# Eight norms of a four-layer fp32 kernel: token half 1 goes to TensorE unscaled, against a diagonal matrix

## The reference

```python
def rms_norm(x, g):
    xf = x.astype(jnp.float32)
    y = xf * lax.rsqrt(jnp.mean(xf * xf, axis=-1, keepdims=True) + RMS_EPS)
    return (y * g.astype(jnp.float32)).astype(x.dtype)
...
h = rms_norm(x, norm_g[l, 0])
...
x = x + rms_norm(h, norm_g[l, 1])
h = conv_ffn(rms_norm(x, norm_g[l, 2]), w_up[l], conv_w[l], conv_b[l], w_down[l])
x = x + rms_norm(h, norm_g[l, 3])
```

## Time and profile before

| | |
|---|---|
| median of 3 runs | 1632.51 us (1631.99 to 1634.74) |
| the profiled execution | 1632.15 us, of which the span of the trace is 1630.4 us |
| TensorE busy | 1531.6 us, 94% of the span |
| VectorE busy | 961.3 us, 59% |
| ScalarE busy | 784.4 us, 48% |
| mean granted TensorE clock | 0.945 of full speed |

### The profile page before, as it was taken

One profiled execution on the slowest core, in us unless ns is written; L12 is line 12 of the kernel. 1 busy time (PEld: TensorE's weight loads), 2 busy tenths in 40 slices (PEclk: granted clock), 3 DMA queues, 4 the chain that ended last, 5 costly groups with the idle time before them and its releaser, 6 DMA issues.

```text
span 1630.4 us, 24600 instructions
## 1 busy us (share of the span) xinstructions
PE 1531.6 (94%) x9621; PEld 1369.2 (84%) x9621; DVE 961.3 (59%) x1438; ACT 784.4 (48%) x1250; POOL 58.2 (4%) x78
## 2 busy tenths in 40 slices
PE   5897999998799998998999989999999999899998
PEld 5865988985699997888999979879999687789997
DVE  6547342235666768556676756575555575655555
ACT  5424321331555557546555656454445455454443
POOL 5002000000000000000000000001000100000000
PEclk9887897996899998999999999999999999999999
DMA  9320000004365553416556545445555445045550
GB/s 290 107 68 0 1 1 1 1 1 143 123 193 193 179 190 129 156 45 215 187 179 201 181 153 183 155 157 181 184 188 195 156 157 179 18 158 188 180 193 39
DMA packets 135063, 222.07 MB, mean 136 GB/s; under 512 B 6137, under 2 KB 105697, under 8 KB 134720
## 3 DMA queue, kind: packets, MB, share of 16 engines
q1 hardware_dynamic: 132688, 214.19, 39.7%
q0 software_dynamic: 2144, 6.61, 1.3%
q10 hardware_dynamic: 144, 0.06, 0.0%
HBM read 219.77 MB, written 1.05 MB: 135 GB/s over the span
## 4 chain that ended last, share of the span: by engine, by line
PE 86%; DVE 8%; ACT 4%; issue 1%; DMA 0%; SPq 0%; DVEq 0%; ACTq 0%
PE ps L446 84%; DVE ulo L432 1%; DVE scratch L1772 1%; PE ps L743 1%; ACT uhi L424 1%; DVE x_sb L1746 1%; DMA raw<-in_w_rkv 0%; DVE scratch L2020 0%; DVE scratch L1852 0%; PE ps L1062 0%; DVE xs L1722 0%; DVE xn_lo L1734 0%; ACT scratch L1290 0%; DVE x_sb L1752 0%; ACT scratch L1388 0%
## 5 line engine op out<-in xcount | busy, mean ns | idle before, releaser
L432 DVE TENSOR_TENSOR ulo<-raw,uhi 128x1024 fp32r<-128x1024 f32 x400 | 492.7, 1235 | 394.6 <-ACT uhi L424 394.3
L424 ACT ACTIVATE uhi<-raw 128x1024 fp32r<-128x1024 f32 x400 | 422.7, 1058 | 449.3 <-PE ps L446 446.3
L446 PE MATMUL ps<-xn_hi,uhi 128*128 128x256 f32 x1472 | 420.6, 286 | 10.7 <-DVE xn_lo L1786 7.7
L446 PE MATMUL ps<-xn_hi,ulo 128*128 128x256 f32 x1472 | 419.3, 285 | 0.0
L446 PE MATMUL ps<-xn_lo,uhi 128*128 128x256 f32 x1472 | 419.2, 285 | 0.0
L446 PEld LDWEIGHTS ps<-xn_hi,uhi 128*128 128x128 f32 x1472 | 285.3, 194 | 14.4 <-issue 9.9
L446 PEld LDWEIGHTS ps<-xn_lo,uhi 128*128 128x128 f32 x1472 | 285.3, 194 | 1.7
L446 PEld LDWEIGHTS ps<-xn_hi,ulo 128*128 128x128 f32 x1472 | 284.8, 193 | 0.0
L446 PE MATMUL ps<-scratch 128*128 128x128 f32 (+6 forms) x1248 | 208.9, 326 | 14.5 <-DVE scratch L2033 9.0
L446 PE MATMUL ps<-uhi,xm_hi 128*128 128x512 f32 x512 | 201.5, 394 | 1.8 <-DVE xm_lo L1968 1.1
L446 PEld LDWEIGHTS ps<-scratch 128*128 128x128 f32 (+3 forms) x1248 | 174.0, 209 | 34.6 <-DVE scratch L2033 10.4
(11 more groups left out here) (271 smaller groups left out, 1420.5 us busy)
## 6 DMA issues: line engine op xcount, KB each, us to landing
raw<-in_mlp_w SPq DMA_DIRECT2D x64, 1024.0 KB, 5.3
raw<-in_w_up SPq DMA_DIRECT2D x44, 1024.0 KB, 5.1
raw<-in_w_down SPq DMA_DIRECT2D x22, 1024.0 KB, 4.8
raw<-in_gmlp_w_in SPq DMA_DIRECT2D x16, 1024.0 KB, 5.2
raw<-in_fox_w_in SPq DMA_DIRECT2D x16, 1024.0 KB, 5.0
raw<-in_w_rkv SPq DMA_DIRECT2D x12, 1024.0 KB, 10.5
raw<-in_gmlp_w_out SPq DMA_DIRECT2D x8, 1024.0 KB, 4.9
raw<-in_w_o_rwkv SPq DMA_DIRECT2D x4, 1024.0 KB, 5.9
```

What stands on the lines that cost most here:

```text
L424: nc.scalar.activation(ring_unit(uhi, m, n), raw_unit(n, j), ACT.Copy).then_inc(hi_done, 1)
L432: nc.vector.tensor_tensor(ring_unit(ulo, m, n), raw_unit(n, j), ring_unit(uhi, m, n).bitcast(F32), ALU.subtract).then_inc(lo_done, 1)
L446: return nc.tensor.matmul(o, l, r, start=start, stop=stop, skip_group_check=True)
```

## The change

For token half 1, DVE no longer writes the scaled half into `xs`. It writes a new 128x128 fp32 tile `diag`, the identity with each row multiplied by that token's reciprocal root. PE then computes for each piece the product of `x_sb` (as the stationary operand, by which it comes out transposed) with `diag`, so that transposing and scaling are one product in fp32. Half 0 stays as it is, a scaling and eight transpositions. `xs_done` counts two events for each norm instead of three.

```diff
+        diag = sb("diag", [P, P])
...
             def norm(n, e):
                 for tok in range(NT):
-                    pe.wait_ge(xs_done, 3 * n + tok + 1)
+                    pe.wait_ge(xs_done, 2 * n + tok + 1)
                     for b in range(4):
-                        if tok == 1 and b == 2:
-                            pe.wait_ge(xs_done, 3 * n + 3)
                         for f in range(2):
                             c = (2 * b + f) * P
-                            last = nc.tensor.transpose(bank(b, P, T * f + P * tok), xs[:, tok, c:c + P], ident[:, :])
+                            o = bank(b, P, T * f + P * tok)
+                            if tok == 0:
+                                nc.tensor.transpose(o, xs[:, 0, c:c + P], ident[:, :])
+                            else:
+                                last = mm(o, x_sb[:, 1, c:c + P], diag[:, :], True, True)
                         if tok == 1:
                             last.then_inc(tr_done, 1)
...
                     step(nc.vector.reciprocal(stat[:, 4 + tok:5 + tok], stat[:, 2 + tok:3 + tok]))
-                    for c in ((slice(0, D),), (slice(0, D // 2), slice(D // 2, D)))[tok]:
-                        TS(xs[:, tok, c], x_sb[:, tok, c], stat[:, 4 + tok:5 + tok], None, ALU.mult).then_inc(xs_done, 1)
+                    if tok == 0:
+                        TS(xs[:, 0, :], x_sb[:, 0, :], stat[:, 4:5], None, ALU.mult).then_inc(xs_done, 1)
+                    else:
+                        TS(diag[:, :], ident[:, :], stat[:, 5:6], None, ALU.mult).then_inc(xs_done, 1)
```

## The result

The changed kernel takes 1640.08 us (median of 6 runs, 1637.65 to 1642.73) against 1631.89 us for the kernel before (6 runs beside it): the ratio is 1.0049, with a 95% interval of 1.0036 to 1.0062, or about 8 us slower. I had forecast 1634.9 us, with a range up to 1638.0. The direction was right. The size, +8.2 us against my +2.4, was more than three times mine.

A forecast was written before the change was run, and what follows sets the result against it. TensorE, busy 1531.6 of 1630.4 us, was taken to bound the kernel. Later first products at the norms, +3.8 us, less 1.4 for a sooner clock made +2.4: 1634.9 us, range 1631.5 to 1638.0.

The forecast's parts named there:

- A product of fp32 leaves two records and costs two transpositions: Half-1 pieces on TensorE: each product takes 0.428 us at low clock or 0.23 at full, against 0.217 and 0.117.
- VectorE's saving is covered: Half-1 scaling: VectorE is 0.63 us ahead, hidden by TensorE's transpositions, and can show only at norms 6 and 7.
- Norm 0 costs nothing: Norm 0: ScalarE's copies of transposed x cover the extra products; 0, up to +0.2 us.
- The sum of +3.8 us over norms 1 to 5 and 7: Later first products: +0.85, +0.84, +0.68, +0.42 and +0.65 us at norms 1 to 5, +0.35 at norm 7.
- The clock gives some back: After norm 2: no idle hole before the products, so full clock returns one 3.4 us stretch sooner; -1.4 us.
- Norm 6, full clock. 0: Norm 6: TensorE's stream ends before the old start of products; 0, between -0.15 and +0.1 us.
- the first (the clock gives nothing back, +3.8 to +5.5): Clock gives nothing back, each norm costs what is listed or a little more; 1636.3 to 1638 us, chance 0.30.
- the second rival: All norms: nothing is hidden, every product's extra counts; +10.3 us, 1642.8 us, chance 0.04 (over +5.5).
- a sign of being wrong: Whole kernel: low-clock time, 5.5% x 2 x 1630, changing by more than one or two stretches would refute the forecast.
- slower by over 0.2%: Whole kernel: a time above 1635.8 us, given chance 0.32.
- The third rival: Five low norms: clock returns a stretch sooner, as products or an unbroken stream count more; -4.7 us, 1627.8, chance 0.06.

The follow-up runs named there:

- transpose_unscaled: The changed kernel with half 1 turned by transpose operations instead of products, its scaling left out; 1630.72 us, ratio 0.9994 to the kernel before.
- diag_0: The kernel before with the change at norm 0 alone; 1632.17 us, ratio 0.9997.
- transpose_twice: The kernel before with each half-1 piece transposed twice in a row; 1635.21 us, ratio 1.0020.
- product_ident: The kernel before with half 1, still scaled by VectorE, turned by fp32 products with the identity at all norms; 1637.72 us, ratio 1.0039.
- diag_6_7: The kernel before with the change at norms 6 and 7 alone; 1632.94 us, ratio 1.0007.
- diag_6: The kernel before with the change at norm 6 alone; 1632.17 us, ratio 1.0007.
- the filled kernels: Kernel before and changed kernel, each with spare identity products ahead of norms 1 to 7; 1625.56 and 1626.78 us (before, two sets), 1626.66 us (changed).
- diag_1_3: The kernel before with the change at norms 1 to 3 alone; 1633.99 us, ratio 1.0010.
- diag_4_7: The kernel before with the change at norms 4 to 7 alone; 1636.29 us, ratio 1.0025.
- the filled changed kernel: The changed kernel with spare identity products into an unread bank ahead of norms 1 to 7; 1626.66 us, ratio 0.9981 to the kernel before.

## Why the prediction was wrong

- **A product of fp32 leaves two records and costs two transpositions: right.** 128 records, 0.209 us each at the low clock.
- **VectorE's saving is covered: right at norms 1 to 5.** `transpose_unscaled` keeps that saving whole, and its stretches 1 to 5 are those of the kernel before to 0.04 us. At norm 6 its first product starts 0.24 us sooner, within the 0.2 to 0.3 that I had for half 1.
- **Norm 0 costs nothing: right** (`diag_0`, ratio 0.9997).
- **The sum of +3.8 us over norms 1 to 5 and 7: right as a sum, and there by luck.** The mean lengths of the stretches over the 11 profiles without fill, with the change or one transposition per piece (so without `transpose_twice` and `product_ident`), with the change at that norm less without it, are +0.71, +0.68, +0.86, +1.04, +0.05 and +0.40: +3.7. Norm 4 cost 0.6 more than its 0.42, because the clock stayed low there for 6.8 us instead of 3.4 in the changed kernel, and norm 5 cost 0.6 less than its 0.65, because there it wasn't low at all. In `product_ident`, where the clock was low at norm 5 too, stretch 5 took 186.7 us, about 1 us more than in the kernel before.
- **"The clock gives some back", -1.4 us: this step failed.** What I foresaw happened in the profile: after norm 2 the clock is back at 648.3 us, 3.6 us sooner after the start of the stretch, and stretch 2 is 0.7 us shorter than before. But norms 4 and 6 each have 3.4 us more at the low clock and norm 5 has 3.4 less, so that with norm 2 the time at the low clock around the norms is 34 us before and after: what one norm gets back another loses. And I had taken one profile of the kernel before for the rule. Among the six profiles without the change at norm 2, stretch 2 took 104.2 to 107.0 us: the kernel gets its clock back early in half of them by itself. One such, `diag_6_7`:

```profile
638.93:743.18 104.25, 91.79 (x584) 81.62 (x584) 65.98 (x160) 61.02 (x152) 0.00 (x0) 0.96 0.30 102
```

  With the change it took 106.3 us in all five. Against the mean of the others, 105.6, the change costs +0.7 at norm 2 instead of giving 0.6.
- **"Norm 6, full clock. 0": this step failed too.** At the full clock it is nothing on the spot: the first product starts 0.04 us later in `diag_6` and in the filled kernels. But the changed kernel met norm 6 at the low clock in all three of its profiles, and the first product came 1.0 to 1.1 us later. The whole stretch, the last attention layer with it, is +2.5 us in the mean of the profiles (standard error 1.1), and `diag_6` alone measured +1.3 (0.7). I had put no term at all for the clock of a layer behind a norm.
- 3.7 + 2.5 + 0.2 (up to norm 1) = 6.4 us by profiles, against 7.2 in the mean of the runs. Taking back the -1.4 and adding norm 6 accounts for most of the miss; the terms after norm 6 and up to norm 1 are known to 1 us at best. Of the rivals, the first (the clock gives nothing back, +3.8 to +5.5) had the mechanism at the norms; its bound of 5.5 was too low, since none of my cases let the clock of a later layer fall. By its number the result lies where I had put the second rival (over +5.5, chance 0.04), but that one's mechanism is not what happened: it wanted 1.7 us at each low norm, and the stretches show at most 1.0.
- I had named as a sign of being wrong that the time at the low clock changes by more than one or two stretches of 3.4 us. It came: 181.7 us in the profile of the kernel before, 202.9 in the first of the changed kernel and 179.6 in the second; by the mean clock of the runs, 0.945 and 0.941, it is 12 to 13 us more. None of that lies at the norms: the first profile has about 13 us more of it up to norm 1 and 10 more behind norm 6.
- Two smaller slips: at norm 4 the clock was back at 945.6 us and not at 945.4, since it had been at the full speed for the first 0.2 us of the window that I read; and the chance for "slower by over 0.2%" should have been at least 0.34, the sum of the first two rivals, where I wrote 0.32.
- The Trainium skill's rule (Perfetto Trace Analysis, Transposes) to use the transpose operation and not a matmul agrees with the runs: the transpose operation in the same place (`transpose_unscaled`) gives the whole loss back. The third rival, by which the clock comes back sooner at the low norms because products count for more than transpositions, gave no gain. `transpose_twice` has stretches 2, 3 and 4 of 106.3, 197.2 and 150.8 us, the changed kernel's are 106.3, 197.3 and 150.9, and the clock was low for as long at each of these norms, so by these profiles the two kinds of work were alike for the clock. The Trainium skill (TensorE: Matmul & The Clock Gate, Part 4) says that transpositions don't count as activity for the clock as matmuls do; these profiles don't agree with it.

What stays open: whether and by what path 1 us of doubled work at a norm brings the clock down 110 us later in the last attention, behind waits that are the same in both profiles; why two doubled transpositions cost less over the whole kernel than products that take as long at the norms; and why the runs of the whole change spread over 12 us where `diag_1_3` and `diag_4_7` spread over 6 and 4 (the filled changed kernel's spread over 14).

## What to carry to other kernels

Ask of a norm or a residual not only which engine is late but at which clock TensorE comes out of the wait: the same doubled fp32 work held up TensorE's next products by 0.7 to 1.2 us where a norm ran at 1.2 GHz, and by 0.04 us or less at 2.4 GHz. Where TensorE is idle for 2 to 5 us ahead of a short critical piece, spare products into an unread bank are worth a try; here they gave 0.2% to 0.4%, more than any edit of the piece itself that was tried. And a difference read from two profiles, one of each kernel, needs a third and fourth of the same kernel before a stretch of it is explained: two stretches here differed by 4 and 6 us between profiles of one kernel.

## What the runs showed of the hardware that was not expected

- The same kernel in two profiles was 10.4 us apart (1641.0 and 1630.6 us of span), with identical instructions; all but 0.7 us of it lay in the two stretches with many short waits of TensorE, up to norm 1 and after norm 6. The other stretches agreed to 0.3 us.
- Between the granted clocks of 0.946 and 0.938, 0.001 of mean clock went with 1.5 us of time in 19 runs of the changed kernel. A run's mean clock is therefore worth reading beside its time.
- Keeping TensorE busy through the five us ahead of norms 1 to 4 left the mean clock of stretches 1, 3 and 4 at 1.00 instead of 0.99, worth 0.5 to 0.7 us each against the profile of before. Stretch 2, at 104.9 us, gained 2.0 against that profile but is 0.7 us longer than in the three unfilled profiles whose clock came back early by itself (104.2 to 104.3).
